# Seven quarter products of sums in place of eight in the second matrix product of a squared-ReLU MLP

## The chip, the cores and the metric

The kernel runs on one core of a Trainium2 chip. The metric is device time in microseconds (us) of one execution. Engines are named as in the profile: PE (TensorE matmul), PEld (its weight loads), DVE (VectorE), ACT (ScalarE), POOL (GpSimd), SP (SyncE, which here only issues DMAs).

## What is computed

One decoder layer on 512 tokens of width 1024: two token mixers, a gated merge, then a squared-ReLU MLP and a last RMSNorm. The change touches the MLP alone:

```python
D_MODEL = 1024
SEQ = 512
D_FF = 4 * D_MODEL
...
        hm = rms_norm(x, mlp_norm_g[l])
        x = x + jnp.square(jax.nn.relu(hm @ w_mlp_in[l])) @ w_mlp_out[l]
    return rms_norm(x, final_norm_g)
```

## The kernel before

All weights stand in DRAM as one stream of slabs of 128x1024 float32 (512 KB). SP loads slab n into one of four buffers `raw`. To multiply float32 numbers, each operand is split in two parts of type fp32r: ACT rounds the slab into `whi` (`hi`, L551), DVE subtracts that from the slab into `wlo` (`lo`, L784), and PE makes three matmuls for each pair of tiles (`three`, L1146 to L1148: high with high, high with low, low with high). Each of `raw`, `whi`, `wlo` has four buffers (`SLOTS`); ACT and DVE work up to three slabs ahead of PE (`AHEAD`).

The hidden width of 4096 is worked in 8 blocks of 512 features. A block (`block_` on each engine, seven of them a hardware loop, the eighth written out by `loop_blocks`) takes eight slabs:

- Slabs 0 to 3: the hidden products. Slab m gives 128 hidden features for all 512 tokens: 8 x 3 = 24 matmuls of 512 columns into bank m (0 to 3) of PSUM. ACT applies ReLU (`rt`, L765), DVE squares (`hv`, L1110), ACT rounds that into `hh` (L767), DVE subtracts into `hl` (L1113).
- Slabs 4 to 7: the output products. They hold the four quarters of the block's 512x1024 output weights, each 256 features by 512 output columns. For each column half, four token tiles of 128 (t) take 4 feature tiles x 3 matmuls each: 96 matmuls in a block. The left half is summed in banks 4 to 7, the right half in banks 0 to 3. After slab 5 and after slab 7 DVE adds the four banks, scaled, to `y` (L1127, `scalar_tensor_tensor`, eight instructions of 128x512 in a block).

The order on each engine is the order in which the code is written; semaphores (`full[b]`: PE has filled bank b, `free[b]`: it has been read out, `hi_done`, `lo_done`, `hv_done`, ...) tie the engines together. POOL has nothing to do within the blocks. After the last block ACT squares `y`, POOL takes the root, DVE scales (`final`) and SP writes the output.

## Time and profile before

| | us |
|---|---|
| median of 3 runs (lowest, highest) | 799.96 (799.68, 801.12) |
| the profiled execution, its own time | 801.33 |
| its span, first to last instruction | 799.4 |
| the eight MLP blocks, from 441.5 to 789.7 of the span | 348.2 |

The profile shows one execution. Its own time is 1.9 us more than its span, and 1.4 us more than the median. In lists of instructions, a row gives the start in us from the beginning of the span, the duration in us, the engine, the line of the code, the operation, output<-inputs and their shapes, and in brackets how long the engine sat idle before and what ended that. A duration is that of one instruction; instructions of one engine overlap a little, so the distance from start to start is shorter: a matmul lasts 0.39 us but the next starts 0.23 us after it.

### The profile page before, as it was taken

How to read it: one execution, taken by the hardware profiler on the slowest of the kernel's cores; microseconds unless marked ns; L12 is line 12 of the kernel's file. 1: busy time of each engine (PE TensorE's matmuls, PEld its weight loads, DVE VectorE, ACT ScalarE, POOL GpSimd, SP SyncE). 2: the span in 40 equal slices, each digit the busy share in tenths (PEclk: the TensorE clock that was granted, in tenths of full speed). 3: DMA queues.
4: the chain of work that ended last, by engine and by line, in shares of the span. 5: the costliest groups of instructions: out<-in, count | busy, mean ns of one | idle time of the engine just before them, and what ended most of it. 6: DMA issues, size and time to landing. Idle time of an engine off the chain costs nothing.

```text
span 799.4 us, 9960 instructions
## 1 busy us (share of the span) xinstructions
PE 763.0 (95%) x3686; PEld 637.8 (80%) x3686; DVE 462.8 (58%) x756; ACT 302.3 (38%) x495; POOL 56.8 (7%) x94
## 2 busy tenths in 40 slices
PE   5999999888997999999999999999999999999995
PEld 4788888777876788888888888888888888888884
DVE  5567878545997897434833644545445454445444
ACT  6453433546632434442421723323232323223231
POOL 3000010011001234400000000000000000000003
PEclk9999999999998999999999999999999999999998
DMA  7522112101322112112352142323323332323202
GB/s 274 159 83 77 53 53 70 62 27 54 98 86 80 54 54 80 53 53 80 118 203 102 53 131 79 105 79 106 104 80 105 104 105 79 105 82 105 76 1 105
DMA packets 20720, 71.46 MB, mean 89 GB/s; under 512 B 2344, under 2 KB 3536, under 8 KB 20688
## 3 DMA queue, kind: packets, MB, share of 16 engines
q1 hardware_dynamic: 19120, 67.88, 25.4%
q10 hardware_dynamic: 1568, 3.15, 1.2%
q8 instruction: 20, 0.33, 0.2%
q14 instruction: 12, 0.10, 0.0%
HBM read 68.91 MB, written 2.11 MB: 89 GB/s over the span
## 4 chain that ended last, share of the span: by engine, by line
PE 84%; DVE 10%; ACT 2%; issue 2%; POOL 0%; DMA 0%; DVEq 0%; ACTq 0%; POOLq 0%; SPq 0%
PE bank L1146 25%; PE bank L1148 24%; PE bank L1147 24%; PE bank L1275 3%; PE bank L1363 2%; DVE sc L940 2%; DVE small L937 2%; PE bank L1154 2%; DVE wlo L784 1%; ACT junk L563 1%; PE bank L1347 1%; PE bank L1161 1%; DVE aqs L834 1%; PE bank L1348 1%; DVE sc L927 1%
## 5 line engine op out<-in xcount | busy, mean ns | idle before, releaser
L784 DVE TENSOR_TENSOR wlo<-raw,whi 128x1024 fp32r<-128x1024 f32 x119 | 146.0, 1228 | 109.8 <-ACT whi L551 104.1
L1146 PE MATMUL bank<-hTh,whi 128*128 128x512 f32 (+1 forms) x456 | 181.2, 397 | 1.4 <-DVE hTl L804 1.4
L1148 PE MATMUL bank<-hTh,wlo 128*128 128x512 f32 (+1 forms) x456 | 178.4, 391 | 0.0
L1147 PE MATMUL bank<-hTl,whi 128*128 128x512 f32 (+1 forms) x456 | 178.4, 391 | 0.0
L551 ACT CAST whi<-raw 128x1024 fp32r<-128x1024 f32 x119 | 124.3, 1045 | 139.2 <-PE bank L1148 139.1
L1146 PEld LDWEIGHTS bank<-hTh,whi 128*128 128x128 f32 (+1 forms) x456 | 85.8, 188 | 21.3 <-issue 2.5
L1148 PEld LDWEIGHTS bank<-hTh,wlo 128*128 128x128 f32 (+1 forms) x456 | 85.7, 188 | 18.7
L1147 PEld LDWEIGHTS bank<-hTl,whi 128*128 128x128 f32 (+1 forms) x456 | 85.9, 188 | 18.5 <-issue 0.7
L1146 PE MATMUL bank<-whi,hh 128*128 128x512 f32 x256 | 99.6, 389 | 0.0
L1147 PE MATMUL bank<-wlo,hh 128*128 128x512 f32 x256 | 99.6, 389 | 0.0
L1148 PE MATMUL bank<-whi,hl 128*128 128x512 f32 x256 | 99.6, 389 | 0.0
L1127 DVE SCALAR_TENSOR_TENSOR y<-bank,small,y 128x512 f32<-128x512 f32 x64 | 46.7, 747 | 25.9 <-PE bank L1148 25.9
L1110 DVE TENSOR_TENSOR hv<-rt 128x512 f32<-128x512 f32 x32 | 22.1, 692 | 67.6 <-ACT rt L765 67.6
L1148 PEld LDWEIGHTS bank<-whi,hl 128*128 128x128 f32 x256 | 48.0, 188 | 10.1
L1146 PEld LDWEIGHTS bank<-whi,hh 128*128 128x128 f32 x256 | 48.0, 188 | 9.9
L1147 PEld LDWEIGHTS bank<-wlo,hh 128*128 128x128 f32 x256 | 48.0, 188 | 9.9
L765 ACT ACTIVATE rt<-bank 128x512 f32<-128x512 f32 x32 | 19.1, 598 | 86.3 <-PE bank L1148 86.3
L1146 PE MATMUL bank<-whi,hTh 128*128 128x512 f32 x96 | 38.9, 405 | 0.0
L1147 PE MATMUL bank<-wlo,hTh 128*128 128x512 f32 x96 | 38.1, 396 | 0.0
L1148 PE MATMUL bank<-whi,hTl 128*128 128x512 f32 x96 | 38.0, 396 | 0.0
L732 ACT ACTIVATE et<-bank 128x128 f32<-128x128 f32 (+3 forms) x32 | 14.0, 436 | 59.5 <-PE bank L1154 59.2
L1113 DVE TENSOR_TENSOR hl<-hv,hh 128x512 fp32r<-128x512 f32 x32 | 22.2, 693 | 22.4 <-ACT hh L767 22.4
(182 smaller groups left out, 1030.5 us busy)
## 6 DMA issues: line engine op xcount, KB each, us to landing
raw<-slabs SPq DMA_DIRECT2D x119, 512.0 KB, 3.3
xs<-x SPq DMA_DIRECT2D x4, 512.0 KB, 4.9
y<-x ACTq DMA_DIRECT2D x1, 2048.0 KB, 9.0
out<-ys SPq DMA_DIRECT2D x3, 512.0 KB, 2.6
bt<-bias_rows ACTq DMA_DIRECT2D x1, 1024.0 KB, 6.0
cst<-consts SPq DMA_DIRECT2D x1, 608.0 KB, 9.8
fg<-final_g SPq DMA_DIRECT2D x1, 512.0 KB, 7.2
out<-ys SPq DMA_DIRECT2D x2, 256.0 KB, 2.1
```

Source lines behind the costliest of these rows:

```text
L551: act.copy(whi[s][:, :], raw[s][:, :]).then_inc(hi_done, 1)
L765: act.activation(rt[m % 2][:, :], bank[m][:, :], ACT.Relu).then_inc(free[m], 1)
L784: dve.tensor_tensor(wlo[s][:, :], raw[s][:, :], whi[s][:, :].bitcast(F32), ALU.subtract).then_inc(lo_done, 1)
L937: dve.max(mx8[:, 8 * (i - 1):8 * i], sc_of(i)).then_inc(S["max_done"], 1)
L940: dve.match_replace(sc_of(i), mx8[:, 8 * (i - 1):8 * i], sc_of(i), TAKEN).then_inc(S["rep_done"], 1)
L1110: dve.tensor_tensor(hv[m % 2][:, :], rt[m % 2][:, :], rt[m % 2][:, :], ALU.mult).then_inc(S["hv_done"], 1)
L1113: dve.tensor_tensor(hl3[:, m, :], hv[m % 2][:, :], hh3[:, m, :].bitcast(F32), ALU.subtract).then_inc(S["hl_done"], 1)
L1127: dve.scalar_tensor_tensor(out=yy, in0=bank[b][:, :], scalar=r2y[:, t:t + 1], in1=yy, op0=ALU.mult, op1=ALU.add).then_inc(free[b], 1)
L1146: pe.matmul(dst, lh, rh, start=start, stop=False)
L1147: pe.matmul(dst, lh, rl, start=False, stop=False)
L1148: return pe.matmul(dst, ll, rh, start=False, stop=stop)
L1275: ins = pe.matmul(bank[bu[0]][:, 64 * v:64 * v + 64].rearrange("p (n h) -> p n h", h=H), un, rhs, start=True, stop=True)
```

## The change

With hidden activations A (512 tokens x 512 features of a block) cut in quarters Art (r: token half, t: feature half), and output weights B cut in Btc (t: feature half, c: column half), seven of the eight blocks now make seven products of quarters instead of eight (`PRODUCTS`; in the order of PE):

| order | left factor | right factor | goes to |
|---|---|---|---|
| 0 | A11 | B11 | banks 0, 1, then `acc1` |
| 1 | A11 - A21 (`sa`) | B22 - B12 (in place in `br12`) | banks 4, 5, kept there over the blocks |
| 2 | A22 | B22 - B12 + B11 - B21 (`wt4`) | banks 2, 3, then `acc4` |
| 3 | A21 + A22 (`sb`) | B12 - B11 (`wt1`) | banks 0, 1, then `acc5` |
| 4 | `sb` - A11 (`sx`) | B22 - `wt1` (`wt2`) | banks 2, 3, then `acc6` |
| 5 | A12 - `sx` (in `sa`) | B22 | banks 0, 1, then `acc3` |
| 6 | A12 | B21 | banks 6, 7, kept there over the blocks |

A product is 256 tokens x 256 features x 512 columns: 2 banks x 2 feature tiles x 3 = 12 matmuls of 512 columns. Their sums, over all seven blocks, give the output quarters once, in the last block, which is itself worked as before (`last_`).

Around this: the four output slabs of a block go to four buffers of their own (`br`), since sums are made of them; the rings `whi`/`wlo` now take 11 slabs a block (4 hidden, 7 factors) instead of 8; the four weight sums (128x1024) and the four activation sums (128x512) are made by POOL; the seven left factors are rounded by ACT (`ah`, in place of 4 `hh`) and their rest is taken by DVE (`al`, in place of 4 `hl`); five products are added by DVE from PSUM to accumulators in SBUF (`gather`, 10 instructions of 128x512 a block, in place of 8 that added to `y`). POOL clears the accumulators before the MLP, and combines them in the last block (5 instructions of 128x1024), where DVE has 10 extra instructions of 128x512. DVE's wait for `ry_done` moves from before the first block to the last one. The core of the diff:

```diff
+PRODUCTS = (1, 7, 4, 5, 6, 3, 2)
...
+        NST = NFB - 1
+        WPB = 4 + len(PRODUCTS)
+        PBANKS = ((0, 1), (4, 5), (2, 3), (0, 1), (2, 3), (0, 1), (6, 7))
+        KEPT = (1, 6)
...
+        def product_full(p, q, it):
+
+            b = PBANKS[p][q]
+            return full[b], it + (MB2[b - 4] + 1) if p in KEPT else out_use(p, q, it) + 1
+
...
+        def a_part(r, c):
+            return hv3[:, 2 * c:2 * c + 2, 256 * r:256 * r + 256]
+
+        def two(t):
+            return t[:, :].rearrange("p (k t) -> p k t", k=2)
+
+        a_src = [a_part(0, 0), two(sa), a_part(1, 1), two(sb), two(sx), two(sa), a_part(0, 1)]
+        w_src = [br["11"], br["12"], wt4, wt1, wt2, br["22"], br["21"]]
+        w_last = [br["11"], br["21"], br["12"], br["22"]]
+        w_last_in = ["11", "21", "12", "22"]
         hh3 = hh[:, :].rearrange("p (k t) -> p k t", k=4)
...
+            def load_out(it):
+                for k, m, after in (("11", 4, WPB - 3), ("12", 6, WPB - 5), ("22", 7, WPB - 1), ("21", 5, WPB)):
+                    sp.wait_ge(lo_done, it * WPB + (NPLAN - WPB + after))
+                    sp.dma_start(br[k][:, :], mlp_slab(m, it)).then_inc(br_in[k], 16)
...
-            with sp.Fori(0, NFB, 1) as it:
-                for m in range(PER_FB):
-                    load(NPLAN + m, it)
+            for m in range(4):
+                load(NPLAN + m)
+            b, u = tiles[n_wo + 7][-1]
+            sp.wait_ge(full[b], u + 1)
+            with sp.Fori(0, NST, 1) as it:
+                load_out(it)
+                for m in range(4):
+                    sp.wait_ge(lo_done, it * WPB + (NPLAN + m + 1))
+                    sp.dma_start(raw[(NPLAN + m) % SLOTS][:, :], mlp_slab(m, it + 1)
+                                 ).then_inc(raw_in[(NPLAN + m) % SLOTS], 16)
+            load_out(NST)
...
+                arrived("11")
+                arrived("12")
+                pool.tensor_tensor(wt1[:, :], br["12"][:, :], br["11"][:, :], ALU.subtract).then_inc(S["wt_done"], 1)
+                arrived("22")
+                stepped("wt_done", 1)
+                pool.tensor_tensor(br["12"][:, :], br["22"][:, :], br["12"][:, :], ALU.subtract).then_inc(S["wt_done"], 1)
+                stepped("hv_done", 2)
+                pool.tensor_tensor(two(sa), a_part(0, 0), a_part(1, 0), ALU.subtract).then_inc(S["s_done"], 1)
+                stepped("wt_done", 2)
+                pool.tensor_tensor(wt2[:, :], br["22"][:, :], wt1[:, :], ALU.subtract).then_inc(S["wt_done"], 1)
+                arrived("21")
+                stepped("wt_done", 3)
+                pool.tensor_tensor(wt4[:, :], wt2[:, :], br["21"][:, :], ALU.subtract).then_inc(S["wt_done"], 1)
+                stepped("hv_done", 4)
+                pool.tensor_tensor(two(sb), a_part(1, 0), a_part(1, 1), ALU.add).then_inc(S["s_done"], 1)
+                stepped("s_done", 2)
+                pool.tensor_tensor(two(sx), two(sb), a_part(0, 0), ALU.subtract).then_inc(S["s_done"], 1)
+                stepped("s_done", 3)
+                pool.wait_ge(S["al_done"], it * 7 + 2)
+                pool.tensor_tensor(two(sa), a_part(0, 1), two(sx), ALU.subtract).then_inc(S["s_done"], 1)
...
+                pool.tensor_tensor(acc[6][:, :], acc[6][:, :], acc[1][:, :], ALU.add).then_inc(S["mix1_done"], 1)
+                pool.tensor_tensor(acc[3][:, :], acc[3][:, :], acc[5][:, :], ALU.add).then_inc(S["mix2_done"], 1)
...
+                act.wait_ge(full[7], it + MB2[3])
+                hi_in(3, it)
+                relu(0, it)
+                act.wait_ge(br_in["11"], it * 16 + 16)
+                hi_out(0, it)
+                relu(1, it)
+                act.wait_ge(S["wt_done"], it * 4 + 2)
+                hi_out(1, it)
+                a_hi(0, it, "hv_done", 2)
+                relu(2, it)
+                act.wait_ge(S["wt_done"], it * 4 + 4)
+                hi_out(2, it)
+                a_hi(1, it, "s_done", 1)
+                relu(3, it)
+                hi_out(3, it)
+                a_hi(2, it, "hv_done", 4)
+                act.wait_ge(*product_full(0, 1, it))
+                hi_out(4, it)
+                a_hi(3, it, "s_done", 2)
+                act.wait_ge(*product_full(1, 1, it))
+                hi_out(5, it)
+                a_hi(4, it, "s_done", 3)
+                act.wait_ge(*product_full(2, 1, it))
+                hi_out(6, it)
+                a_hi(5, it, "s_done", 4)
+                a_hi(6, it, "hv_done", 4)
+                act.wait_ge(*product_full(4, 1, it))
+                hi_in(0, it + 1)
+                act.wait_ge(*product_full(5, 1, it))
+                hi_in(1, it + 1)
+                act.wait_ge(*product_full(6, 1, it))
+                hi_in(2, it + 1)
...
+            def square_relu(m, it):
+                dve.wait_ge(free[m], in_use(m, it) + 1)
+                r_ = rt[m % 2][:, :]
+                dve.tensor_tensor(hv3[:, m, :], r_, r_, ALU.mult).then_inc(S["hv_done"], 1)
+            def a_lo(k, it):
+                dve.wait_ge(S["ah_done"], it * 7 + (k + 1))
+                dve.tensor_tensor(two(al[k]), a_src[k], two(ah[k]).bitcast(F32), ALU.subtract).then_inc(S["al_done"], 1)
+            def gather(p, it):
+                for q in range(2):
+                    b = PBANKS[p][q]
+                    dve.wait_ge(*product_full(p, q, it))
+                    a_ = acc[PRODUCTS[p]][:, q * T:(q + 1) * T]
+                    dve.tensor_tensor(a_, bank[b][:, :], a_, ALU.add).then_inc(free[b], 1)
+            def block_(it):
+                lo_in(3, it)
+                square_relu(0, it)
+                lo_out(0, it)
+                square_relu(1, it)
+                lo_out(1, it)
+                a_lo(0, it)
+                square_relu(2, it)
+                lo_out(2, it)
+                a_lo(1, it)
+                square_relu(3, it)
+                lo_out(3, it)
+                a_lo(2, it)
+                gather(0, it)
+                a_lo(3, it)
+                lo_out(4, it)
+                a_lo(4, it)
+                lo_out(5, it)
+                gather(2, it)
+                a_lo(5, it)
+                a_lo(6, it)
+                lo_out(6, it)
+                gather(3, it)
+                gather(4, it)
+                lo_in(0, it + 1)
+                gather(5, it)
+                lo_in(1, it + 1)
+                lo_in(2, it + 1)
...
+            def block_(it, begin=False, end=False):
+                for m in range(4):
+                    hidden(m, it)
+                for p in range(len(PRODUCTS)):
+                    s = (NPLAN + 4 + p) % SLOTS
+                    wh, wl = slab_view(whi, s, 2), slab_view(wlo, s, 2)
+                    kept = p in KEPT
+                    pe.wait_ge(lo_done, it * WPB + (NPLAN + 4 + p + 1))
+                    pe.wait_ge(S["al_done"], it * 7 + (p + 1))
+                    for q in range(2):
+                        b = PBANKS[p][q]
+                        if not kept:
+                            pe.wait_ge(free[b], out_use(p, q, it))
+                        elif begin:
+                            pe.wait_ge(free[b], MB2[b - 4])
+                        for kk in range(2):
+                            ins = three(bank[b][:, :], two(ah[p])[:, kk, q * P:(q + 1) * P],
+                                        two(al[p])[:, kk, q * P:(q + 1) * P], wh[:, kk, :], wl[:, kk, :],
+                                        (begin or not kept) and kk == 0, (end or not kept) and kk == 1)
+                        ins.then_inc(full[b], 1)
...
+            block_(0, begin=True)
+            with pe.Fori(1, NST - 1, 1) as it:
+                block_(it)
+            block_(NST - 1, end=True)
+            last_(NST)
```

How it stands in the engines' queues. First POOL between the preparation of `r2y` and the end of the kernel; before the change it goes from there straight to the sums of the last RMSNorm:

```order
L478 TENSOR_TENSOR small_65<-small_65 128x4
L534 TENSOR_TENSOR small_65<-small_65 128x4
L538 TENSOR_TENSOR small_65<-small_65 128x1
```

In the changed kernel, one turn of the loop (`hv` is the squared ReLU, the other names are in the table above):

```order
L601 TENSOR_TENSOR wt1_132<-br12_124,br11_123 128x1024
L597 ISA
L604 TENSOR_TENSOR br12_124<-br22_126,br12_124 128x1024
L597 REGISTER_ALU
L606 TENSOR_TENSOR sa_135<-hv_122 128x512
L608 TENSOR_TENSOR wt2_133<-br22_126,wt1_132 128x1024
L597 REGISTER_ALU
L611 TENSOR_TENSOR wt4_134<-wt2_133,br21_125 128x1024
L597 REGISTER_ALU
L613 TENSOR_TENSOR sb_136<-hv_122 128x512
L615 TENSOR_TENSOR sx_137<-sb_136,hv_122 128x512
L617 ISA
L618 TENSOR_TENSOR sa_135<-hv_122,sx_137 128x512
```

Eight instructions of two inputs from SBUF are new on POOL in each of seven turns. Next DVE from the last square of a block to the end of the first half of the output products, before:

```order
L1110 TENSOR_TENSOR hv1_123<-rt1_121 128x512
L1112 REGISTER_ALU
L1113 TENSOR_TENSOR hl_119<-hv1_123,hh_118 128x512
L783 REGISTER_ALU
L784 TENSOR_TENSOR wlo2_59<-raw2_51,whi2_55 128x1024
L783 REGISTER_ALU
L784 TENSOR_TENSOR wlo3_60<-raw3_52,whi3_56 128x1024
L1122 REGISTER_ALU
L1127 SCALAR_TENSOR_TENSOR y_116<-bank4,small_65,y_116 128x512
L1127 SCALAR_TENSOR_TENSOR y_116<-bank5,small_65,y_116 128x512
```

And now, from the last square over the gathering of product 0:

```order
L1287 TENSOR_TENSOR hv_122<-rt1_121 128x512
L1275 REGISTER_ALU
L1276 TENSOR_TENSOR wlo2_59<-wt1_132,whi2_55 128x1024
L1290 REGISTER_ALU
L1291 TENSOR_TENSOR al2_147<-hv_122,ah2_140 128x512
L1297 REGISTER_ALU
L1299 TENSOR_TENSOR acc1_127<-bank0,acc1_127 128x512
L1299 TENSOR_TENSOR acc1_127<-bank1,acc1_127 128x512
L1290 REGISTER_ALU
L1291 TENSOR_TENSOR al3_148<-sb_136,ah3_141 128x512
L1275 REGISTER_ALU
L1276 TENSOR_TENSOR wlo3_60<-wt2_133,whi3_56 128x1024
```

It goes on in the same way to the gathering of product 3, which must be done before PE may begin product 5 in the same banks:

```order
L1291 TENSOR_TENSOR al4_149<-sx_137,ah4_142 128x512
L1275 REGISTER_ALU
L1276 TENSOR_TENSOR wlo0_57<-br22_126,whi0_53 128x1024
L1297 REGISTER_ALU
L1299 TENSOR_TENSOR acc4_128<-bank2,acc4_128 128x512
L1299 TENSOR_TENSOR acc4_128<-bank3,acc4_128 128x512
L1290 REGISTER_ALU
L1291 TENSOR_TENSOR al5_150<-sa_135,ah5_143 128x512
L1290 REGISTER_ALU
L1291 TENSOR_TENSOR al6_151<-hv_122,ah6_144 128x512
L1275 REGISTER_ALU
L1276 TENSOR_TENSOR wlo1_58<-br21_125,whi1_54 128x1024
L1297 REGISTER_ALU
L1299 TENSOR_TENSOR acc5_129<-bank0,acc5_129 128x512
```

Between the last square and that gathering stand now four rests of weights, five rests of activations and four gathering instructions; before, from the last square to the last addition of the first half, there stood one rest of activations, two of weights and four additions.

## Rows read from the trace of the kernel before

**Rows 1.** The page: busy time, share of the span and instructions by engine.
```profile
span 799.4 us, 9960 instructions
PE 763.0 (95%) x3686; PEld 637.8 (80%) x3686; DVE 462.8 (58%) x756; ACT 302.3 (38%) x495; POOL 56.8 (7%) x94
```

**Rows 2.** Busy time by block; PEclk is the granted clock; sum over all eight.
```profile
core 0: us, PE busy (x) PEld busy (x) DVE busy (x) ACT busy (x) POOL busy (x), PEclk, DMA share, GB/s
485.00:528.60 43.60, 43.60 (x194) 36.12 (x193) 20.99 (x24) 12.92 (x16) 0.00 (x0) 1.00 0.30 97
sum 348.20, PE 348.20 PEld 288.19 DVE 167.77 ACT 111.20 POOL 3.23; mean PE 43.52 PEld 36.02 DVE 20.97 ACT 13.90 POOL 0.40
```

**Rows 3.** Timeline where a hidden tile ends and its evictions begin.
```profile
490.36 0.39 PE L1148 MATMUL bank<-hTh,wlo 128*128 128x512 f32 x1
490.58 0.39 PE L1146 MATMUL bank<-hTh,whi 128*128 128x512 f32 x1
490.78 0.60 ACT L765 ACTIVATE rt<-bank 128x512 f32<-128x512 f32 x1 [4.38 <-PE bank L1148]
491.41 0.69 DVE L1110 TENSOR_TENSOR hv<-rt 128x512 f32<-128x512 f32 x1 [3.76 <-ACT rt L765]
492.14 0.63 ACT L767 ACTIVATE hh<-hv 128x512 fp32r<-128x512 f32 x1 [0.76 <-DVE hv L1110]
```

**Rows 4.** DVE timeline, output products of the same block: start to start.
```profile
513.63 1.23 DVE L784 TENSOR_TENSOR wlo<-raw,whi 128x1024 fp32r<-128x1024 f32 x1 [2.33 <-ACT whi L551]
514.77 1.40 DVE L1127 SCALAR_TENSOR_TENSOR y<-bank,small,y 128x512 f32<-128x512 f32 x2
```

**Rows 5.** Groups on DVE and ACT: count | busy, mean ns of one.
```profile
L784 DVE TENSOR_TENSOR wlo<-raw,whi 128x1024 fp32r<-128x1024 f32 x119 | 146.0, 1228 | 109.8 <-ACT whi L551 104.1 <-POOL small L534 5.3
L1113 DVE TENSOR_TENSOR hl<-hv,hh 128x512 fp32r<-128x512 f32 x32 | 22.2, 693 | 22.4 <-ACT hh L767 22.4
L1075 DVE TENSOR_TENSOR obl<-bank,obh 128x512 fp32r<-128x512 f32 x4 | 2.5, 684 | 5.2 <-ACT obh L581 5.2
L551 ACT CAST whi<-raw 128x1024 fp32r<-128x1024 f32 x119 | 124.3, 1045 | 139.2 <-PE bank L1148 139.1 <-DMA raw<-slabs 0.2
```

**Rows 6.** Groups on POOL: the two sizes of its two-input instruction.
```profile
L525 POOL TENSOR_TENSOR bm<-bt,sc 128x256 f32<-128x256 f32 x24 | 17.6, 735 | 18.7 <-DVE small L1058 18.6
L525 POOL TENSOR_TENSOR bm<-bt,sc 128x128 f32<-128x128 f32 x8 | 3.6, 459 | 45.2 <-ACT bt L722 28.3 <-DVE small L1058 16.9
```

**Rows 7.** POOL and DVE at the same time, both with SBUF inputs only (POOL: two copies).
```profile
L492 POOL COPY kd<-c0s x2: 612/1108/1603, 101.5 to 102.0; 128x512 f32<-128x512 f32 x2
101.47 2.16 POOL L492 COPY kd<-c0s 128x512 f32<-128x512 f32 x2
101.57 1.59 DVE L784 TENSOR_TENSOR wlo<-raw,whi 128x1024 fp32r<-128x1024 f32 x1
103.09 1.63 DVE L965 TENSOR_TENSOR hX<-hF 128x1024 f32<-128x1024 f32 x1
104.64 1.22 DVE L966 TENSOR_TENSOR hX<-hF 128x1024 f32<-128x1024 f32 x1
```

**Rows 8.** POOL and DVE at the same time, DVE reading PSUM and one SBUF input.
```profile
293.36 0.61 POOL L524 TENSOR_SCALAR bm<-sc,bt 128x128 f32<-128x128 f32 x1
293.57 0.56 DVE L1058 CUSTOM_DVE_ANT_0 tt<-bank,bm 128x384 f32<-128x384 f32 x1
293.93 0.74 POOL L525 TENSOR_TENSOR bm<-bt,sc 128x256 f32<-128x256 f32 x1
```

**Rows 9.** PE after idle times, and the granted clock in a stretch behind the first.
```profile
161.04 0.39 PE L1263 MATMUL bank<-ikh,iqs 128*128 128x256 f32 x1 [1.72 <-ACT hKT L693]
162.78 0.63 PE L1147 MATMUL bank<-wlo,hTh 128*128 128x512 f32 x1
162.40:165.70 3.30, 3.30 (x9) 2.60 (x8) 2.64 (x4) 1.64 (x3) 0.00 (x0) 0.50 0.00 0
238.08 1.10 PE L1332 MATMUL bank<-bt,cst 128*128 128x512 f32 x2 [1.32 <-DVE oal L804]
239.72 0.39 PE L1146 MATMUL bank<-hTh,whi 128*128 128x512 f32 x1
```

**Rows 10.** The page, DMA issues: KB each, us from issue to landing.
```profile
raw<-slabs SPq DMA_DIRECT2D x119, 512.0 KB, 3.3
xs<-x SPq DMA_DIRECT2D x4, 512.0 KB, 4.9
```

More of the change, by code:

```diff
@@ L338, in build, with used_up @@
         BY_COUNT = seen
[L340 to L350 removed]
+        def used_up(n):
             if n in by_count:
@@ L530, in _ @@
                     do_side(s)
+            b, u = tiles[n_ub + 3][-1]
+            pool.wait_ge(full[b], u + 1)
+            for p in acc:
+                pool.memset(acc[p][:, :], 0.0).then_inc(S["acc_zero"], 1)
             pool.wait_ge(S["sq_done"], SQ_Y + NT)
@@ L757, in _ @@
                 square(y3[:, t, :], D, ssy[:, t:t + 1])
-            def block_(it, last):
-                for m in range(PER_FB):
-                    if not (last and m + AHEAD >= PER_FB):
-                        hi(NPLAN + m + AHEAD, it)
-                    if m < 4:
-                        act.wait_ge(full[m], it * 2 + (MB + 1))
-                        act.activation(rt[m % 2][:, :], bank[m][:, :], ACT.Relu).then_inc(free[m], 1)
-                        act.wait_ge(S["hv_done"], it * 4 + (m + 1))
-                        act.activation(hh3[:, m, :], hv[m % 2][:, :], ACT.Copy).then_inc(S["hh_done"], 1)
@@ L769, in _, with hi_in, hi_out, relu @@
-            loop_blocks(act, block_)
+            def hi_in(m, it):
+                s = (NPLAN + m) % SLOTS
+                act.wait_ge(raw_in[s], it * 16 + 16 * ((NPLAN + m) // SLOTS + 1))
+                act.copy(whi[s][:, :], raw[s][:, :]).then_inc(hi_done, 1)
+            def hi_out(k, it):
+                s = (NPLAN + 4 + k) % SLOTS
+                act.copy(whi[s][:, :], w_src[k][:, :]).then_inc(hi_done, 1)
+            def relu(m, it):
+                act.wait_ge(full[m], in_use(m, it) + 1)
+                if m >= 2:
+                    act.wait_ge(S["hv_done"], it * 4 + (m - 1))
+                act.activation(rt[m % 2][:, :], bank[m][:, :], ACT.Relu).then_inc(free[m], 1)
@@ L1423, in _, with hidden @@
-            loop_blocks(pe, block_)
+            def hidden(m, it):
+                s = (NPLAN + m) % SLOTS
+                wh, wl = slab_view(whi, s, KD_), slab_view(wlo, s, KD_)
+                pe.wait_ge(lo_done, it * WPB + (NPLAN + m + 1))
+                pe.wait_ge(free[m], in_use(m, it))
+                for q, k in enumerate(MLP_K):
+                    if m == 0:
+                        pe.wait_ge(free[k], mlp_bank[k][1] + 1)
+                    ins = three(bank[m][:, :], wh[:, k, :], wl[:, k, :], hTh3[:, k, :], hTl3[:, k, :],
+                                q == 0, q == KD_ - 1)
+                ins.then_inc(full[m], 1)
```

244 lines of the change are left out of this document (154 added, 90 removed).

## The prediction

> **What bounds the kernel now.** I read the page first: PE is busy 95% of the span, DVE 58%, ACT 38%, POOL 7% [rows 1]. Then the busy times by block: in all eight MLP blocks PE has no idle time, its clock is at the full level (granted 1.00, 2.4 GHz), and a block takes 43.5 us [rows 2]. DVE works 21.0 us of a block, ACT 12.9, POOL nothing. So in this stage, 348 of the 799 us, time is the number of matmuls times their distance. That distance is 43.52 / 192 = 0.227 us; one alone lasts 0.39 us [rows 3], which must not be taken as its price. Nothing in the MLP waits for DMA.
>
> **What is removed.** A product of quarters has 12 matmuls; one is gone from each of seven blocks: 7 x 12 x 0.227 = **19.0 us**. All are on the path. A changed block is 180 x 0.227 = 40.8 us at best, a hidden tile in it 5.44 us, a product 2.72 us. The last block is as before.
>
> **What is added, by engine.** DVE gets 11 weight rests, 4 squares, 7 activation rests and 10 gathers a block. By [rows 5]: 11 x 1.23 + 11 x 0.69 + 10 x 0.68 = 27.9 us. ACT: 11 x 1.05 + 4 x 0.60 + 7 x 0.63 = 18.4 us. POOL: two sizes are known, 0.46 us at 128 columns and 0.735 at 256 [rows 6], thus 2.16 ns a column; straight on this gives 1.29 us at 512 and 2.39 us at 1024 columns, four of each a block: 14.7 us. No average comes near 40.8 us. But the work isn't spread: the seven products take 19.0 us, and in them stand four of the weight rests for them, five activation rests and all gathers.
>
> **A walk through one block, engines independent.** Time 0 is the end of the fourth hidden tile. Start to start, a weight rest takes 1.14 us and is followed by the next [rows 4]; of the 0.69 us instructions I take 0.60. The last square starts at 0.85 (0.2 for the last matmul to end, 0.60 for ReLU [rows 3]). From there DVE needs, up to the first half of the gathering of product 3: square 0.60, four weight rests 4.56, five activation rests 3.00, four gather instructions 2.40, one more to its end 0.69: 11.25 us, so 12.1. PE wants those banks for product 5 at 5 x 2.72 = 13.6. Product 4 wants the banks of product 2 at 10.9; by the same steps they are free at 8.6. The sums reach ACT in time (`sb` at 1.6 + 1.3 = 2.9, `sx` 4.2, `sa` 5.5; their rests are due at 8.2, 10.9 and 13.6). PE would not wait, and the whole 19.0 us would stay. The margin is 1.5 us.
>
> **They aren't independent.** [Rows 7] show it: a POOL copy from SBUF to SBUF starts at 101.47 and takes 0.61 us; a DVE subtraction of two SBUF tensors issued at 101.57 takes 1.59 us instead of 1.22, and ends as if it had begun when the copy was nearly over. The second copy, issued at 102.03, takes 1.60 instead of 0.61: it waits until that subtraction is over. The next subtraction takes 1.63, the one after, with POOL silent, 1.22. So one holds the other up for the whole instruction, in turn. A DVE instruction with PSUM as one input isn't held up: 0.56 us with POOL busy on both sides of it [rows 8]. All squares and rests read SBUF twice, the gathers don't.
> The Trainium skill (SBUF — State Buffer, section "Who interferes with whom") says the same as a rule: VectorE instructions with two SBUF inputs and GpSimd instructions that read SBUF take turns at a shared port pair under an exclusive lock, and the loser blocks fully. No row here shows it for POOL's `tensor_tensor`, which this change uses; the trace agrees for the copy. By the rule the sum is the one below, without it the first rival's.
> The Trainium skill (GPSIMD Engine Reference, section "3.1 Elementwise — side-by-side cycle accounting") gives 4497 ns for a 2048-column `tensor_tensor`; an estimate of half would be 2.25 us at 1024 columns, near my 2.39.
>
> **The same walk with turns taken.** I let POOL go 0.13 us before its recorded end and DVE 0.14, as in [rows 7]. Before time 0, POOL makes `sa`, `wt2`, `wt4` from -9.3 on (after the second square); DVE's rests between them hold it up, `wt4` ends at about -1.9 instead of -3.2, and `wlo` of it and `al1` come late: the last square starts at 1.0. Then `sb` holds up the next weight rest by 1.1 us, `sx` the rest `al2` by 1.1; `sa` runs beside gathers and costs nothing. `wt1` of the next block (2.39 us) comes when its two slabs have landed: requested when the rest of `wt1` is read at about 4, they need 3.3 us for the first and about 4.9 for the second, as the rows of lone and of crowded 512 KB loads say [rows 10], so about 9. If it gets in before `al4` (due at 8.7) it holds DVE up by 2.2 us; the first half of the gathering of product 3 then ends at 12.1 + 0.2 + 1.1 + 1.1 + 2.2 = 16.7, and product 5, due at 13.6, starts **3.3 us** late with PE's restart. If it gets in after the following weight rest, it runs beside the gathers of product 2 and holds up only `al5` by 1.0: end at 15.5, **2.2 us** late with the restart and the late product 2. I can't tell which; the two differ by 0.3 us of arrival. So 2.2 to 3.3 us a block, middle 2.8, times 7 = **19.6 us** given back, between 15 and 24. A block then takes some 43.6 us, as before.
> Behind product 6 comes the hidden phase, 21.8 us in which DVE has 8 us of work: the delay doesn't pass on, but comes again in each block.
>
> **PE's clock.** An idle time of 1.72 us was followed within 1.7 us by matmuls of 0.63 us instead of 0.39 at a granted clock of 0.50 (1.2 GHz), for 3.3 us at least, so 1.7 us lost; one of 1.32 us was not [rows 9]. Here PE's idle times are 0.7 to 1.7 us each, of two or three a block. The rows bound it from 0 to 7 falls, 0 to 12 us. I take 2 falls, 3.4 us, since most idle times are below the one that did it.
>
> **Small terms.** POOL's clearing of accumulators lies in the output projection, where POOL is idle and the fills only write: 0. `ry_done` moves out of the way of the first block, where PE didn't wait for it: 0. Last block: 10 more DVE instructions, 7 us, and five of 2.39 on POOL, 12 us, beside 21.8 us of hidden tiles; the rests for its second output slab are due at 27: 0, at worst 2 us. DMA: as many slabs as before. ACT's longer queue has 1 us or more of lead at each rounding. After the MLP nothing is changed.
>
> **Sum.** Profiled execution: 801.33 - 19.0 + 19.6 + 3.4 = 805.3. It was 1.4 us over the median of its runs, so a median of **803.9**. With both bounds: from 801.3 - 19.0 + 15 - 1.4 = 796 to 801.3 - 19.0 + 24 + 5 - 1.4 = 810.
>
> **Rivals.**
> *No turns taken, or hardly any* (other side). If POOL's `tensor_tensor` doesn't block DVE as its copy did, or lets go early, PE never waits and the time is 801.3 - 19.0 - 1.4 = 780.9. Deciding point: held up by less than 1.5 us in all between the last square and the gathering of product 3, and the gain is whole. With half of the 4.4 us that I count, the gathering ends at 14.3 and PE waits about 0.9 us a block: 787. For it: only a copy is shown, and POOL's two-input loop may leave pauses that DVE can use. Against it: POOL's copy held DVE from start nearly to end. It has 0.27, half of that at 781.
> *Turns taken, and the clock falls in nearly every block.* Idle times of 1.7 us, as in the row that was followed by a fall: 24 + 12 instead of 19.6 + 3.4 gives up to 817. POOL instructions longer than the straight line, with strided inputs, lead there too: each 0.1 us more at 1024 columns adds 0.2 to 0.3 us a block. It has 0.16.
> *The change doesn't do what it says* (PE makes as many matmuls): the code has 84 fewer; nothing for it.
>
> **Chances.** Forecast (turns taken, 796 to 810) 0.57, first rival (781 to 796) 0.27, second (810 to 817) 0.16. A measurement of this kernel tells about 0.2% from no change, 1.6 us, so "same" is 798.4 to 801.6. Of the forecast's 0.57, 0.12 lie below, 0.12 within, 0.33 above. Faster 0.39, same 0.12, slower 0.49. The range 780 to 810 holds 0.84; leaving out the second rival, and nothing of the first, whose likeliest value stands at its very end.
>
> **What would show each step.** PE: 84 matmuls fewer, still 0.227 us apart; seven blocks of 43 to 44 us, with idle times before products 4 or 5 put down to DVE's `acc`. DVE: weight rests and activation rests in the products above 1.3 and 0.8 us, up to 2.9 and 2.9; gathers at 0.69 throughout. POOL: `wt` instructions of 2.4 us alone, up to 3.4 when they wait. The forecast is wrong if rests beside POOL last 1.23 and 0.69, if PE's blocks are 40.8 us, or if the idle times lie elsewhere: before a hidden tile (ACT late) or product 2 (POOL's `wt4` late by over 5 us).

## The result and the profile after

| | before | changed |
|---|---|---|
| median, us (lowest, highest) | 799.96 (799.68, 803.58) | 812.8 (812.33, 817.67) |
| the profiled execution, its own time | 801.33 | 817.67 |
| its span | 799.4 | 815.9 |

The changed kernel is slower: 1.0171 times the time before, 95% interval 1.0151 to 1.0191, or 12.8 us. I had predicted 803.9 us, with a range up to 810; 812.8 stands 2.8 us above it. The direction was the likelier one (slower, 0.49), the size was off. The profiled execution is 4.9 us over its median, so rows of it add up to more than the 12.8 us. Most of that lies ahead of the MLP, where this execution had the lower granted clock for longer than the others (0.95 in the mean from 100 to 200 us, 0.97 to 1.00 in every other trace here): its MLP begins at 443.85 us, that of e4 and e5 below, with the same program up to there, at 439.5.

The page of the changed kernel, its busy times and the costliest group of the seven products' matmuls. They answer to [rows 1]: 84 matmuls fewer on PE, a quarter more busy time on DVE, POOL at 204 us.

```profile
PE 756.4 (93%) x3602; PEld 626.2 (77%) x3602; DVE 582.5 (71%) x824; ACT 333.4 (41%) x537; POOL 204.3 (25%) x160
...
L1400 PE MATMUL bank<-whi,ah 128*128 128x512 f32 x196 | 79.2, 404 | 19.6 <-DVE acc L1299 17.1
```

The busy times by stretch, where [rows 2] had 43.5 us and a DVE at 21.0: two turns of the loop, each from hidden tile to hidden tile, the first with a fall of the clock in it.

```profile
core 0: us, PE busy (x) PEld busy (x) DVE busy (x) ACT busy (x) POOL busy (x), PEclk, DMA share, GB/s
542.35:587.18 44.83, 42.54 (x181) 34.76 (x180) 35.70 (x32) 17.44 (x23) 18.30 (x8) 0.96 0.28 93
587.18:631.40 44.22, 41.41 (x181) 33.63 (x180) 35.64 (x32) 17.44 (x23) 17.79 (x8) 1.00 0.28 95
```

A block has 180 matmuls instead of 192, yet lasts 44.2 us instead of 43.5. DVE is busy for 35.6 us of it, where I had added up 27.9 us of work. PE's idle times, from its timeline (the first two are of block 0, in which one of the three is left out; the next two of block 1; then one of block 2; the last stands in the last block):

```profile
470.60 0.47 PE L1400 MATMUL bank<-whi,ah 128*128 128x512 f32 x1 [1.98 <-DVE wlo L1276]
482.63 0.69 PE L1400 MATMUL bank<-whi,ah 128*128 128x512 f32 x1 [2.88 <-DVE acc L1299]
527.60 0.50 PE L1400 MATMUL bank<-whi,ah 128*128 128x512 f32 x1 [2.29 <-DVE acc L1299]
531.13 0.50 PE L1400 MATMUL bank<-whi,ah 128*128 128x512 f32 x1 [0.50 <-DVE acc L1299]
571.80 0.79 PE L1400 MATMUL bank<-whi,ah 128*128 128x512 f32 x1 [2.29 <-DVE acc L1299]
787.96 0.80 PE L1400 MATMUL bank<-whi,hh 128*128 128x512 f32 x1 [3.65 <-DVE hl L1340]
```

A bracket is a little less than what the idle time adds to the distance of two matmuls. By distances, block 0 lost 5.8 us, blocks 1 to 5 lost 2.45 us ahead of product 4 and 0.65 ahead of product 5 (in block 2 only the first), block 6 lost 1.0: 21.8 us in seven blocks. The last block lost 3.8 us.

Where the 16.5 us between the two spans are:

| | us |
|---|---|
| the MLP starts later (443.85 instead of 441.48): chance of the two executions, see above | +2.4 |
| 84 matmuls fewer | -19.0 |
| idle times in the seven blocks | +21.8 |
| idle time in the last block | +3.8 |
| matmuls at half clock behind three of the idle times, and distances a little over 0.227 us behind the others | +7.6 |
| sum | +16.6 |

Row five is what is left of the MLP's 14.1 us over before. In it, 24 matmuls listed 0.43 us apart instead of 0.227 make 4.8 us, and the distance from the first matmul behind an idle time to the second, longer by 0.1 us, or by 0.3 to 0.4 where the clock falls, makes another 2.3.

Block 0 lost more than the others by a wait of its own. POOL begins its first sum 9.5 us after the start of that block (453.33), while in the later blocks that sum is made before the block starts. So its last weight sum (`wt4`) comes late, and ACT, which rounds it, is held up:

```profile
467.59 1.05 ACT L868 CAST whi<-wt 128x1024 fp32r<-128x1024 f32 x1 [5.99 <-POOL wt L611]
```

The rounding for product 1 stands behind that in ACT's queue; this is the first PE row above.

What made PE wait is in DVE's timeline of block 2, whose fourth hidden tile ends at about 558.5:

```profile
561.38 1.78 DVE L1291 TENSOR_TENSOR al<-hv,ah 128x512 fp32r<-128x512 f32 x1
563.09 1.28 DVE L1299 TENSOR_TENSOR acc<-bank,acc 128x512 f32<-128x512 f32 x2
564.88 2.31 DVE L1276 TENSOR_TENSOR wlo<-wt,whi 128x1024 fp32r<-128x1024 f32 x1
567.12 2.89 DVE L1291 TENSOR_TENSOR al<-sx,ah 128x512 fp32r<-128x512 f32 x1
569.93 1.21 DVE L1276 TENSOR_TENSOR wlo<-br,whi 128x1024 fp32r<-128x1024 f32 x1
571.07 1.28 DVE L1299 TENSOR_TENSOR acc<-bank,acc 128x512 f32<-128x512 f32 x2
```

and in POOL's of the same stretch:

```profile
560.25 2.36 POOL L613 TENSOR_TENSOR sb<-hv 128x512 f32<-128x512 f32 x1 [3.63 <-DVE hv L1287]
562.69 1.63 POOL L615 TENSOR_TENSOR sx<-sb,hv 128x512 f32<-128x512 f32 x1
564.49 1.63 POOL L618 TENSOR_TENSOR sa<-hv,sx 128x512 f32<-128x512 f32 x1 [0.17 <-POOL sx L615]
566.54 2.92 POOL L601 TENSOR_TENSOR wt<-br,br 128x1024 f32<-128x1024 f32 x1 [0.43 <-DMA br<-slabs]
574.67 2.40 POOL L604 TENSOR_TENSOR br<-br,br 128x1024 f32<-128x1024 f32 x1 [5.21 <-DMA br<-slabs]
```

This is the pattern of [rows 7], for the instruction that the change uses. `al<-sx` is 0.68 us of work (its sister `al<-sb` takes 0.677 in the mean) and lasts 2.89, since POOL's `wt1` runs from 566.54 to 569.46. `sb` is 1.29 us of work and lasts 2.36, since it waits for DVE's. The additions from PSUM, 0.68 us each, lie across POOL's instructions and aren't held up, as with the PSUM input in [rows 8]. POOL's `wt1` was the case "in before `al4`": its second slab landed 8 us after the end of the last hidden tile. The last row is POOL alone: 2.40 us at 1024 columns, where my straight line gave 2.39.

### The profile page after: what moved, and what is told of

The parts are those of the page before. It is cut to its first block, busy times and chain, and to the rows that moved or that the text cites. A ratio compares the mean times of both kernels' runs of the same rounds, so it can differ in the third digit from the quotient of the medians.

```text
span 815.9 us, 10129 instructions
## 1 busy us (share of the span) xinstructions
PE 756.4 (93%) x3602; PEld 626.2 (77%) x3602; DVE 582.5 (71%) x824; ACT 333.4 (41%) x537; POOL 204.3 (25%) x160
## 4 chain that ended last, share of the span: by engine, by line
PE 64%; DVE 19%; issue 8%; ACT 5%; POOL 2%; DMA 1%; DVEq 0%; SPq 0%; ACTq 0%; POOLq 0%
PE bank L1400 18%; PE bank L1401 18%; PE bank L1402 18%; DVE wlo L1276 3%; PE bank L1529 3%; DVE al L1291 3%; PE bank L1617 2%; DVE acc L1299 2%; DVE sc L1110 2%; DVE small L1107 2%; PE bank L1408 2%; DVE wlo L954 2%; ACT junk L663 1%; DVE y L1332 1%; DMA xs<-x 1%
## 5 line engine op out<-in xcount | busy, mean ns | idle before, releaser
L954 DVE TENSOR_TENSOR wlo<-raw,whi 128x1024 fp32r<-128x1024 f32 x58 | 71.2, 1230 | 45.9 <-ACT whi L651 45.6
L1400 PE MATMUL bank<-whi,ah 128*128 128x512 f32 x196 | 79.2, 404 | 19.6 <-DVE acc L1299 17.1
L1401 PE MATMUL bank<-wlo,ah 128*128 128x512 f32 x196 | 77.5, 395 | 0.0
L1402 PE MATMUL bank<-whi,al 128*128 128x512 f32 x196 | 77.4, 395 | 0.0
L651 ACT CAST whi<-raw 128x1024 fp32r<-128x1024 f32 x58 | 60.5, 1044 | 29.6 <-PE bank L1402 29.4
L1400 PEld LDWEIGHTS bank<-whi,ah 128*128 128x128 f32 x196 | 37.5, 191 | 32.8 <-DVE acc L1299 17.3
L863 ACT CAST whi<-raw 128x1024 fp32r<-128x1024 f32 x29 | 29.8, 1050 | 70.4 <-PE bank L1402 70.4
L1276 DVE TENSOR_TENSOR wlo<-br,whi 128x1024 fp32r<-128x1024 f32 x32 | 52.2, 1630 | 4.3 <-ACT whi L868 3.5
L1276 DVE TENSOR_TENSOR wlo<-raw,whi 128x1024 fp32r<-128x1024 f32 x29 | 37.8, 1323 | 16.6 <-ACT whi L863 16.3
L1299 DVE TENSOR_TENSOR acc<-bank,acc 128x512 f32<-128x512 f32 x70 | 44.2, 678 | 0.0
L1402 PEld LDWEIGHTS bank<-whi,al 128*128 128x128 f32 x196 | 37.5, 191 | 8.2
L1401 PEld LDWEIGHTS bank<-wlo,ah 128*128 128x128 f32 x196 | 37.7, 192 | 7.5
```

The costliest lines, as they stand in the source:

```text
L651: act.copy(whi[s][:, :], raw[s][:, :]).then_inc(hi_done, 1)
L863: act.copy(whi[s][:, :], raw[s][:, :]).then_inc(hi_done, 1)
L954: dve.tensor_tensor(wlo[s][:, :], raw[s][:, :], whi[s][:, :].bitcast(F32), ALU.subtract).then_inc(lo_done, 1)
L1276: dve.tensor_tensor(wlo[s][:, :], src[:, :], whi[s][:, :].bitcast(F32), ALU.subtract).then_inc(lo_done, 1)
L1299: dve.tensor_tensor(a_, bank[b][:, :], a_, ALU.add).then_inc(free[b], 1)
L1400: pe.matmul(dst, lh, rh, start=start, stop=False)
```

## The experiments

All are compared with runs of the kernel before on the same chip (799.85 to 800.66 us there).

### The blocks: is it turns, and which ones?

**e1_wt1_later.** POOL makes the next block's `wt1` only when DVE has made three of the rests for its hidden tiles, behind all rests of this block's products.

```diff
+                pool.wait_ge(lo_done, it * WPB + (NPLAN + 3))
                 arrived("11")
                 arrived("12")
```

> One POOL instruction moved: POOL begins wt1 of the next block only when DVE has made the last weight rest of that block's third hidden slab, some 18 us before it would next be needed, instead of as soon as its two slabs land (8 us behind the last hidden tile, beside the rest al4). Theory of turns (POOL's and DVE's instructions with two SBUF inputs wait for each other): al4 falls from 2.9 to 0.69 us, the 2.45 us of PE idle time before product 4 goes, about 1.2 us a block stays from sb and sx; 11 to 13 us less than the changed kernel's 812.8, so about 801. Rival (DVE simply has too many instructions in the products, and POOL's place does not matter): DVE has the same queue, so 812 to 813.

Measured: 800.68 us, 0.9998 [0.9984, 1.0012] of before, so 12.1 us less than the changed kernel, by one wait on an engine that has time. `wt1` now starts 15 us later in the block. The mean of `al<-sx` fell from 2261 ns to 678, and blocks 1 to 5 have one idle time of 0.67 us each:

```profile
L1292 DVE TENSOR_TENSOR al<-sx,ah 128x512 fp32r<-128x512 f32 x6 | 4.1, 678 | 0.0
```

In its trace the blocks' second idle time, ahead of product 5, is what stayed, and only one fall of the clock is left, in the last block. So the collision of this one POOL instruction with one DVE instruction was 2.4 of the 3.1 us that a block lost.

**e2_sums_on_dve.** The eight sums of a block are DVE's, and POOL has nothing to do in the seven blocks.

```diff
             def block_(it):
                 lo_in(3, it)
+                w_sum(1, it)
+                w_sum(2, it)
                 square_relu(0, it)
...
                 a_lo(0, it)
+                a_sum(0, it)
+                w_sum(3, it)
+                w_sum(4, it)
...
                 square_relu(3, it)
+                a_sum(1, it)
                 lo_out(3, it)
                 a_lo(2, it)
+                a_sum(2, it)
                 gather(0, it)
                 a_lo(3, it)
+                a_sum(3, it)
```

> All eight sums of a block are made by DVE, POOL is silent within the seven blocks; the last block is as in the changed kernel. Theory of turns: nothing holds DVE up, every rest takes 1.23 or 0.69 us, DVE's work rises from 28 to 35 us a block, yet PE's idle time falls from 22 us in all to about 5 (0.7 a block, before product 5); with one or two falls of the clock less the time is 792 to 796. Rival (too much work on DVE): three more 0.6 us instructions stand ahead of the gathering of product 3, 1.8 us more idle time in each of seven blocks, so 824 or more.

Measured: 793.16 us, 0.9904 [0.9872, 0.9937]. DVE has eight more instructions a block, and PE's idle time a block fell from 3.1 to 0.45 us. Rests and squares are as short as before the change:

```profile
L1250 DVE TENSOR_TENSOR wlo<-br,whi 128x1024 fp32r<-128x1024 f32 x24 | 29.3, 1222 | 2.9 <-ACT whi L842 2.9
L1261 DVE TENSOR_TENSOR hv<-rt 128x512 f32<-128x512 f32 x24 | 16.6, 690 | 34.1 <-ACT rt L848 34.1
L1265 DVE TENSOR_TENSOR al<-hv,ah 128x512 fp32r<-128x512 f32 x18 | 12.3, 685 | 0.0
```

**e5_gather_early.** The other suspect was the order: the gathering of product 3 stands behind two rests that product 5 doesn't need.

```diff
                 a_lo(5, it)
+                gather(3, it)
                 a_lo(6, it)
                 lo_out(6, it)
-                gather(3, it)
```

> The changed kernel with one step of DVE's order moved: the gathering of product 3 stands before the last activation rest and the last weight rest of the products instead of behind them, so that the banks for product 5 come free 1.8 us earlier in the queue. POOL is as in the changed kernel. Theory of turns: the rests held up by sb, sx and wt1 stand ahead of the gathering of product 2, which is as late as before, and the weight rest for product 6 is now late in place of the gathering: 810 to 813.5. Rival (the order of DVE's queue is the fault, POOL a minor one): the idle times of 3.1 us a block shrink by 1 us or more, 805 or less.

Measured: 812.18 us, 1.0148 [1.0119, 1.0177]. The order isn't the main fault: the 2.45 us ahead of product 4 stays in each block, only the 0.67 us behind it went. The seven blocks have nearly 5 us less idle time in this trace (16.9), and the time hides that, since it has five falls of the clock in the MLP instead of three: 42 matmuls about 0.43 us apart instead of 24, 3.6 us more.

### Is it POOL's time, its reading, or its writing?

**e3_pool_writes.** POOL fills instead of summing: it writes as much as the sums do or more, for as long or longer, and reads next to nothing (for a weight sum three such fills, each behind a subtraction of one column). The kernel leaves the sums out and takes quarters themselves as factors, so its output isn't the layer's; all waits stay.

```diff
-                pool.tensor_tensor(wt1[:, :], br["12"][:, :], br["11"][:, :], ALU.subtract).then_inc(S["wt_done"], 1)
+                pool.memset(spare[:, 0:1024], 0.0).then_inc(S["spare_step"], 1)
...
+                pool.tensor_tensor(small[:, 251:252], rsx[:, 0:1], rsx[:, 0:1], ALU.subtract).then_inc(S["wt_done"], 1)
```

> The eight sums are left out (quarters themselves are taken as factors, so the output is not the reference's) and POOL instead fills spare memory for about as long: three memsets of 1024 columns for a weight sum, one of 1024 and one of 512 for an activation sum, with tiny instructions between that carry the waits. All waits of the other engines stay. Theory of turns over reading: POOL is as busy but reads nothing of size, DVE's rests take 1.23 and 0.69 us, no idle time of PE in the seven blocks, 786 to 790. Rival (any POOL work slows DVE, or the idle time comes from waiting for POOL's results): rests stay stretched or idle times stay, 808 to 813.

Measured: 815.79 us, 1.0172 [1.0152, 1.0192]: neither of the two times that I had expected, and the experiment had two causes in it. DVE was not held up, as the theory had it (rests 1221 ns, `al` 688, squares 691). But three fills with their steps between take 3.5 us, not 2.4, POOL fell behind, and now ACT waited for it. ACT's timeline:

```profile
556.55 1.05 ACT L938 CAST whi<-br 128x1024 fp32r<-128x1024 f32 x1 [4.87 <-POOL small L659]
```

So the time says nothing of reading or writing; e7 has a shorter chain.

**e7_pool_writes_short.** The same with two fills of 1024 columns for a weight sum and one for an activation sum; it leaves the sums out as e3 does.

> As the kernel in which POOL fills memory instead of making sums (left out, quarters taken as factors), but with fills of the sums' own length: two memsets of 1024 columns (2.3 us) for a weight sum, one (1.2 us) for an activation sum. The longer fills had DVE unstretched, but ACT waited for POOL's longer chain. Theory of turns over reading: POOL busy some 14 us a block, DVE at 1.22 and 0.69 us, and its results in time: idle times below 0.7 us a block, 786 to 792 (the last block keeps its 3.6 us). Rival (what counts is that POOL's results come late, not the reading): 805 or more.

Measured: 792.52 us, 0.9898 [0.9869, 0.9927]. That is 0.5 us over the top of what I expected; the blocks from the second on have no idle time over 0.25 us, and what is left is 2.7 us in block 0 and 4.7 us in the last block, which stays as changed, each with slow matmuls behind it. POOL's fills and DVE's rests, in the same stretch:

```profile
L617 POOL MEMSET spare<- 128x1024 f32 x5 | 4.8, 958 | 0.0
...
L1322 DVE TENSOR_TENSOR wlo<-br,whi 128x1024 fp32r<-128x1024 f32 x36 | 44.0, 1221 | 17.2 <-ACT whi L914 17.2
...
L1337 DVE TENSOR_TENSOR al<-hv,ah 128x512 fp32r<-128x512 f32 x35 | 23.5, 683 | 3.6 <-ACT ah L924 3.6
```

A busy POOL that only writes holds nothing up; what does is the sums' reading of SBUF. One reservation: a fill is also another instruction than a sum, and no run has a sum that doesn't read.

**e8_before_with_pool.** The other way round: the kernel before, with eight subtractions a block on POOL for which nobody waits.

```diff
+                pool.tensor_tensor(spare[:, 0:cols], hTh[:, 0:cols].bitcast(F32), hTl[:, 0:cols].bitcast(F32),
+                                   ALU.subtract).then_inc(S["spare_step"], 1)
```

> The kernel before, with POOL added beside it in seven blocks: four subtractions of 128x1024 and four of 128x512, inputs hTh and hTl, output in spare memory, two groups released by the second and the fourth square of a block as in the changed kernel; nobody waits for them. Theory of turns: DVE's rests and squares are stretched here too, by up to 2.4 us, but the queue has 22 us of slack in a block and the eight instructions of PE's banks are due later, so PE has no or little idle time: 800 to 802. Rival (turns cost PE wherever POOL reads): 1 us or more a block, 807 or more.

Measured: 801.8 us, 1.0013 [0.9997, 1.003]. DVE is slowed as expected, and the time doesn't show it. DVE's and POOL's groups, six blocks:

```profile
L805 DVE TENSOR_TENSOR wlo<-raw,whi 128x1024 fp32r<-128x1024 f32 x46 | 87.8, 1908 | 23.2 <-ACT whi L572 23.2
L1148 DVE SCALAR_TENSOR_TENSOR y<-bank,small,y 128x512 f32<-128x512 f32 x44 | 31.3, 743 | 7.5 <-PE bank L1169 7.5
L1131 DVE TENSOR_TENSOR hv<-rt 128x512 f32<-128x512 f32 x24 | 29.7, 1236 | 33.8 <-ACT rt L786 33.8
```

```profile
L539 POOL TENSOR_TENSOR spare<-hTh,hTl 128x1024 f32<-128x1024 f32 x24 | 69.9, 2914 | 1.9
L539 POOL TENSOR_TENSOR spare<-hTh,hTl 128x512 f32<-128x512 f32 x24 | 38.2, 1593 | 149.5 <-DVE hv L1131 148.5
```

A rest goes from 1.22 to 1.91 us, a square from 0.69 to 1.24; the addition with a PSUM input stays at 0.743. Turns by themselves cost this kernel nothing measurable. They cost in the changed one, where I had reckoned DVE's lead at 1.5 us.

### The last block

**e4_last_on_dve.** The five combinations of accumulators are DVE's, four of them behind its last rests. The six additions to `y` that use their results go behind those rests too, so the edit changes two things at once.

```diff
-                pool.tensor_tensor(acc[6][:, :], acc[6][:, :], acc[1][:, :], ALU.add).then_inc(S["mix1_done"], 1)
-                pool.tensor_tensor(acc[3][:, :], acc[3][:, :], acc[5][:, :], ALU.add).then_inc(S["mix2_done"], 1)
...
+                dve.tensor_tensor(acc[6][:, :], acc[6][:, :], acc[1][:, :], ALU.add).then_inc(S["mix1_done"], 1)
...
                 square_relu(3, it)
                 h_lo(3)
                 w_lo(3)
+                dve.tensor_tensor(acc[3][:, :], acc[3][:, :], acc[5][:, :], ALU.add).then_inc(S["mix2_done"], 1)
```

> Only the last block is changed: the five combinations of accumulators are made by DVE, four of them and the additions to y behind the last rests of that block. Theory of turns for the last block: the 3.65 us that PE waits for hl before the output products goes, and with it the fall of the clock behind it (3.4 us): 6 to 7 us less, 806 to 807. Rival (the idle time is DVE's own ten additional instructions): they are still there, so 811 to 813.

Measured: 808.53 us, 1.009 [1.0066, 1.0115], 4.3 us less than the changed kernel, between my two cases. The profiled execution is the fastest of the four (805.57). In it the blocks' idle times are nearly as in the changed kernel (block 0 lost 5.0 us), one fall of the clock stands in block 0, and the last block has no idle time and no slow matmul.

**e10_blocks_only** and **e6_all** make the same comparison where nothing else is wrong. e6_all is e2, e4 and e5 together; e10_blocks_only is e6_all with the last block as in the change. (`e6_all` ran first.)

> Three edits together: all sums on DVE, the gathering of product 3 earlier, and the last block's combinations on DVE behind its rests. Theory of turns: no stretched instruction is left; the 0.45 us before product 5 that the kernel with sums on DVE has in each of seven blocks goes, since the gathering comes 1.8 us earlier; the 3.65 us and the fall of the clock in the last block go too. 793.2 - 3.2 - 3.6 - 1.7 = 784.7, at best the whole gain of 84 matmuls, 781. Rival (something else bounds the blocks below 43.5 us, ACT or the DMAs): idle times appear elsewhere, 788 or more.

> e6_all (781.0 us) with the last block put back as in the changed kernel: the five combinations of 128x1024 on POOL, everything in the seven blocks as in e6_all. This prices the prediction's small term for the last block (0, at worst 2 us) by itself. Theory: POOL's three combinations hold DVE's rests up in turn, PE waits 3.8 us ahead of the last block's output products and its clock is at half for 6.8 us behind that (3.4 us lost): 781.0 + 7.2 = 788.2, and the trace has no other idle time. Rival: the last block cost that much in the changed kernel only because DVE came into it late from the block before; then it costs 0 to 2 us here: 781 to 783.

Measured: e6_all 781.04 us (780.29 to 783.94), 0.975 [0.9722, 0.9778]; e10_blocks_only 786.34 us, 0.9826 [0.9807, 0.9845]. The last block as changed costs 5.3 us by these medians, where I had priced it at 0, at worst 2. They are of two chips; set against the kernel before on each, it is 6.1 us, and in the two traces the last block differs by 5.9. The 7.2 that I then expected of e10 was too much, since I had counted 6.8 us of low clock as 3.4 us lost. In e10, PE idles 4.2 us, and 8 matmuls 0.43 us apart lose 1.6. PE's row behind that idle time, DVE's timeline around it, and POOL's:

```profile
758.12 0.50 PE L1421 MATMUL bank<-whi,hh 128*128 128x512 f32 x1 [4.01 <-DVE hl L1360]
```

```profile
739.72 2.12 DVE L1360 TENSOR_TENSOR hl<-hv,hh 128x512 fp32r<-128x512 f32 x1 [0.70 <-ACT hh L908]
741.75 3.41 DVE L1250 TENSOR_TENSOR wlo<-br,whi 128x1024 fp32r<-128x1024 f32 x1
...
757.38 0.69 DVE L1360 TENSOR_TENSOR hl<-hv,hh 128x512 fp32r<-128x512 f32 x1 [0.70 <-ACT hh L908]
```

```profile
738.56 2.72 POOL L606 TENSOR_TENSOR acc<-wt,acc 128x1024 f32<-128x1024 f32 x1 [3.34 <-DVE wt L1373]
741.24 2.85 POOL L607 TENSOR_TENSOR acc<-wt,acc 128x1024 f32<-128x1024 f32 x1
```

`wlo` takes 3.41 us instead of 1.22 and `hl` 2.12 instead of 0.69; from there DVE is behind, and the six additions to `y` that the change puts between its last squares (4.0 us) keep it there. PE's last hidden matmul starts at 747.60, and 27 output matmuls follow, the last at 753.72. The 28th is the first that needs the fourth tile's `hl`, and that starts at 757.38, 3.7 us after the 27th. The two rows shown are 3.6 us of holding up; how much would stay with the combinations on DVE but the six additions where they are, no run tells.

e6_all beats both kernels by far. It has no idle time of PE in the MLP, and a block takes what 180 matmuls take:

```profile
490.00:531.00 41.00, 41.00 (x183) 33.95 (x182) 33.14 (x41) 17.44 (x23) 0.00 (x0) 1.00 0.31 104
```

It is 19.6 us faster than the kernel before: the whole of the 84 matmuls. And DVE is busy for 33.1 us a block, with the eight sums, less than the 35.6 us in the changed kernel, without them. A block of e7_pool_writes_short, where DVE neither makes the sums nor is held up, gives the third number, 26.1:

```profile
490.00:530.90 40.90, 40.90 (x182) 33.89 (x181) 26.13 (x32) 17.24 (x22) 17.56 (x32) 1.00 0.32 104
```

The eight sums cost DVE 33.1 - 26.1 = 7.0 us a block when it makes them, and 35.6 - 26.1 = 9.5 us when POOL does. (The windows are 0.1 to 0.2 us longer than a block of 40.8 us; over exactly one block e6_all has 32.9.)

**e9_pool_placed.** Is there a place for POOL at all? The changed kernel with e1, e4 and e5.

> The changed kernel with all eight sums of a block still on POOL, but placed: the first weight sum of the next block starts only after the weight rests of the products (as in e1_wt1_later), the gathering of product 3 stands ahead of the last rests (as in e5_gather_early), and the five combinations of the last block are on DVE (as in e4_last_on_dve). e1_wt1_later ran 800.7 us, with 0.67 us of idle time a block ahead of product 5 (seven times 0.67 = 4.7) and 3.8 us of idle time in the last block with 3.4 us of slow clock behind it. If the fault is where POOL's sums stand, not that POOL makes them, both go: 800.7 - 4.7 - 7.2 = 788.8, or as low as 784 if the first block's idle times (4.3 us) go too. If POOL beside DVE costs whatever the place (the remaining held-up rests wlo beside sx and al2 beside sa), idle times stay in each block and the time is 793 or more. The kernel with everything on DVE (e6_all) ran 781.0.

Measured: 788.44 us, 0.9846 [0.9824, 0.9868]. PE's idle times are 2.16 us in block 0 (with 8 matmuls at half clock behind it) and 0.34 or less in the others, though squares last 1730 ns. So the changed kernel becomes 24.4 us faster with all eight sums of a block still on POOL. Some 6 of these belong to the last block, whose combinations went to DVE; most of what the seven blocks had lost was a matter of where the instructions stand. Not all of it: e6_all is 7.4 us faster still. Of that, block 0 makes 4.0 us (44.9 us here, 40.9 there) and the six blocks behind it 0.4 us each. One of those blocks here:

```profile
484.00:525.30 41.30, 41.22 (x182) 33.80 (x181) 35.24 (x33) 17.55 (x23) 18.53 (x8) 1.00 0.30 104
```

## Why the prediction was wrong

- **What is removed**: right. Where PE doesn't wait (e6_all) the time is 780.3 to 783.9, and I had 780.9 for that case.
- **The work by engine**: POOL's prices were right (1.29 us at 512 columns, 2.40 at 1024). DVE's 27.9 us holds only with POOL silent or filling (26.1; durations overlap a little).
- **Turns**: right in what is held up (`tensor_tensor` with two SBUF inputs: yes; from PSUM: no). The term was 19.6 us, between 15 and 24; it was 21.8. Of my two cases for `wt1` it was the one at 3.3 us a block; blocks 1 to 5 lost 3.1, but most of it ahead of product 4, for which I hadn't added up the same delays (8.6 + 4.6 = 13.2, where PE is due at 10.9). That the sum of all seven fits so well is partly luck: I had priced them alike, and block 0 lost 5.8 us, 2 of them by POOL's late sums, and block 6, with no `wt1` of a next block, 1.0. The first rival, without turns, is out. The Trainium skill (SBUF — State Buffer, section "Who interferes with whom") says that a VectorE instruction with two SBUF inputs contends with a GpSimd instruction that reads SBUF, not with one that only writes it. The runs agree in both halves: e8 with 1.91 us for 1.22, e7 with 1.221 beside fills.
- **Where it failed: the last block.** I set 10 more DVE instructions, 7 us, and five on POOL, 12 us, beside 21.8 us of hidden tiles, looked only at when the weight rest of its second output slab is due, and put the term at 0, at worst 2 us. That is a sum of averages, of the kind that I had refused for the other blocks, where I walked from instruction to instruction with turns taken. It cost 5.3 to 6.1 us by e10 against e6_all, and 6.5 us in the profiled execution (3.8 us of idle time, the rest slow matmuls). The wait was for DVE's last `hl`, which I hadn't looked at. POOL's instructions held DVE up for 2.2 + 1.4 us at the two rows shown of e10, and that `hl` stands behind twelve added instructions in DVE's queue, not ten: two additions to `y` from banks 6 and 7 were missing from my count, here and in the description of the change.
- **The clock**: I took 2 falls for 3.4 us. In the seven blocks of the profiled execution there were two, in blocks 0 and 2, for 3.2 us; the third stands in the last block and goes with its idle time. They followed idle times of 3.0, 2.4 and 3.8 us; I had reckoned with idle times of 0.7 to 1.7. The number 2 was a guess, and e5, with four in seven blocks, shows that it could have come out otherwise.
- **The sum**: 812.8 is 8.9 over the forecast. The two profiled executions show where: the MLP was to be 4.0 us longer (-19.0 + 19.6 + 3.4) and is 14.1. Of these 10.1 us too many, the last block is 6.5, the blocks' idle times are 2.2 (21.8 for 19.6), and the rest is mostly the longer first distances behind idle times. The medians, 1.3 us closer together than the two MLPs, can't be split further.
- **The second rival** (810 to 817) holds the measured time, but by another mechanism: it wanted clock falls in nearly every block, and there were two in seven.

The range failed by the same step: it took the bounds of the block term and the clock, and for the last block 2 us in words and none in numbers.

## What to carry to other kernels

Work given to POOL was free here only where DVE wasn't reading two SBUF tensors at the same time, or where DVE had lead: the eight sums cost DVE more from POOL (9.5 us a block) than on DVE itself (7.0), and one of them, started 15 us later, was worth 12 us. Before offloading, write down what each instruction of both engines lies beside, in the last and the first turn of a loop too, not only in its middle. And where a stretch is added up from averages "beside 21.8 us of other work", look at which instruction the next stage waits for and what now stands ahead of it.
